# Up-projections of a hybrid decoder step: the first of four weight sums made by a plain and an accumulating transfer

## What is computed

```python
def conv_ffn(x, buf, w_up, conv_w, w_down):
    hc, new_buf = causal_dwconv(x @ w_up, conv_w, buf)     # w_up: (1024, 5632)
    return (jax.nn.silu(hc[..., D_FF:]) * hc[..., :D_FF]) @ w_down, new_buf
```

## Time and profile before

| | |
|---|---|
| median of three runs | 1750.44 us (1749.59 to 1751.86) |
| profiled execution, own time | 1752.5 us |
| its span in the trace | 1749.1 us |
| TensorE busy (matmul) | 1715.6 us, 98% of the span |
| VectorE busy | 1088.8 us, 62% |
| ScalarE busy | 460.1 us, 26% |
| GpSimd busy | 254.5 us, 15% |
| 16 DMA engines | 24% busy, 139.36 MB, 80 GB/s |

### The profile page before, as it was taken

How to read it: one execution, slowest core, us unless ns; L and a number is a source line. 1 busy time by engine, 2 the same in 40 slices (tenths; PEclk the granted TensorE clock), 3 DMA queues, 4 the chain that set the end, 5 groups by cost and what they waited for, 6 DMA issues and landing times. The chain is left out here.

```text
span 1749.1 us, 22019 instructions
## 1 busy us (share of the span) xinstructions
PE 1715.6 (98%) x7827; PEld 1334.3 (76%) x7827; DVE 1088.8 (62%) x2090; ACT 460.1 (26%) x1084; POOL 254.5 (15%) x540
## 2 busy tenths in 40 slices
PE   8999999999899999999999999999999999999999
PEld 6777778877677777777777777777677777777777
DVE  4766775667867666672437655467666667632365
ACT  2433407730422222220014101114222222200051
POOL 0111216762210000000100000002000000001100
PEclk9999999999999999999999999999999999999999
DMA  4232210312122222241130223211222222322211
GB/s 153 73 114 86 80 61 14 110 52 106 48 82 77 83 73 73 85 154 66 67 110 25 96 85 94 73 50 49 61 84 73 73 85 80 129 101 74 82 53 55
DMA packets 45644, 139.36 MB, mean 80 GB/s; under 512 B 4945, under 2 KB 12241, under 8 KB 45537
## 3 DMA queue, kind: packets, MB, share of 16 engines
q1 hardware_dynamic: 42864, 133.36, 23.1%
q10 hardware_dynamic: 2672, 4.61, 0.8%
HBM read 129.63 MB, written 8.31 MB: 79 GB/s over the span
## 5 line engine op out<-in xcount | busy, mean ns | idle before, releaser
L274 PE MATMUL bank<-z,ring 128*128 128x288 f32 x1952 | 508.7, 407 | 6.9 <-DVE z L392 2.3
L274 PEld LDWEIGHTS bank<-z,ring 128*128 128x128 f32 x1952 | 371.1, 191 | 113.4 <-issue 5.1
L274 PE MATMUL bank<-x,ring 128*128 128x288 f32 x1632 | 429.7, 410 | 10.5 <-DMA x<-in_x 4.8
L274 PEld LDWEIGHTS bank<-x,ring 128*128 128x128 f32 x1632 | 311.2, 192 | 101.8 <-issue 6.7
L2188 DVE SCALAR_TENSOR_TENSOR scratch<-scratch 128x592 f32<-128x592 f32 x176 | 146.2, 832 | 25.6 <-ACT scratch L2132 24.0
L274 PE MATMUL bank<-y,ring 128*128 128x288 f32 x616 | 156.7, 406 | 0.3 <-DVE x L1949 0.3
L274 PEld LDWEIGHTS bank<-y,ring 128*128 128x128 f32 x616 | 117.0, 190 | 33.0 <-issue 0.7
L274 PE MATMUL bank<-big,ring 128*128 128x288 f32 x536 | 137.0, 411 | 2.7 <-issue 1.1
L274 PEld LDWEIGHTS bank<-big,ring 128*128 128x128 f32 x536 | 102.4, 192 | 33.1 <-issue 3.4
L2222 POOL COPY scratch<-scratch 128x2 f32<-128x2 f32 x88 | 26.5, 301 | 467.7 <-ACT scratch L2118 467.7
L2132 ACT ACTIVATE scratch<-scratch 128x592 f32<-128x592 f32 x88 | 69.4, 789 | 90.6 <-DVE scratch L2162 89.0
(11 more groups left out here) (377 smaller groups left out, 2236.3 us busy)
## 6 DMA issues: line engine op xcount, KB each, us to landing
ring<-in_w_up SPq DMA_DIRECT2D x88, 512.0 KB, 3.5
ring<-in_w_scin SPq DMA_DIRECT2D x24, 512.0 KB, 3.6
ring<-in_w_qkv SPq DMA_DIRECT2D x21, 512.0 KB, 3.5
ring<-in_w_down SPq DMA_DIRECT2D x12, 704.0 KB, 4.3
scratch<-in_w_down SPq DMA_DIRECT2D x12, 704.0 KB, 5.3
ring<-in_w_z SPq DMA_DIRECT2D x8, 512.0 KB, 3.5
big<-in_st_S SPq DMA_DIRECT2D x16, 256.0 KB, 5.6
out_dn_S_sample<-big SPq DMA_DIRECT2D x16, 256.0 KB, 2.3
```

The lines of the kernel that those rows point to most:

```text
L274: last = pe.matmul(bank[:, 0:HALF], w[:, k * P:(k + 1) * P], rhs(k), start=start and k == 0, stop=k == self.depth - 1, skip_group_check=no ...
```

## The change

s1 of sets 2 to 21 of each layer isn't made by VectorE any more. SP copies a21 from memory to the place of s1 as soon as `p5` of set i - 2 has read the old one (one more 256 KB transfer, ahead of the set's two others). When it has landed (`s1_first`), POOL issues a transfer of a22 from memory that adds to what is there (`accum_op=ALU.add`), which increments `s1_added`. VectorE waits for `s1_added` ahead of `sum2`, and signals `sum1_made` itself behind it. In POOL's queue the transfer for set i stands first in its turn, and `history_out` and `history_in` of a set have moved one turn later in the loop. Sets 0 and 1 keep `sum1`, `sum2` and `sum3`. The names in the diff: `s1_uses` counts the uses of a semaphore.

```diff
--- before.py
+++ after.py
@@ -360,6 +360,14 @@
                 if g >= 2 and not (self.own_blocks and i >= 2):
                     dve.wait_ge(product6, g - 1)
                 dve.tensor_tensor(w["s2"], w["s1"], w["a11"], ALU.subtract).then_inc(sum2_made, 1)
+
+            def sum2_of_loaded(self, dve, i):
+                g, w = self.base + i, self.weights(i)
+                dve.wait_ge(*self.loaded(i, "a11"))
+                dve.wait_ge(*self.loaded(i, "a21"))
+                dve.wait_ge(product6, g - 1)
+                dve.tensor_tensor(w["s2"], w["s1"], w["a11"], ALU.subtract).then_inc(sum2_made, 1)
+                dve.sem_inc(sum1_made, 1)
 
             def sum3(self, dve, i):
                 w = self.weights(i)
@@ -1811,6 +1819,7 @@
             phase_sem(f"ple_{x}") for x in ("projected", "projected_out", "sigmoids", "gate", "out", "p_in"))
         sc_ch, sc_samples, sc_hist, sc_tap0, sc_tap1, sc_conv, sc_made, sc_saved, sc_pads, sc_in = (
             phase_sem(f"sc_{x}") for x in ("ch", "samples", "hist", "tap0", "tap1", "conv", "made", "saved", "pads", "in"))
+        s1_first, s1_added = ([phase_sem(f"s1_{x}{n}") for n in range(2)] for x in ("first", "added"))
         big_loaded = [phase_sem(f"big_loaded{n}") for n in range(4)]
         chunk_loaded = [[phase_sem(f"chunk{s}_{x}_loaded") for x in ("a11", "a12", "a21", "a22")] for s in range(2)]
 
@@ -2800,13 +2809,13 @@
             f.tap(dve, 0, 1, 2)
             f.tap(dve, 0, 0, 1)
             f.tap(dve, 0, 0, 2)
-            d.sum1(dve, 2)
             for i in range(2, FT):
                 p = i - 1
                 if i > 2:
                     f.u2(dve, p)
                 f.c22(dve, p)
-                d.sum2(dve, i)
+                dve.wait_ge(s1_added[i % 2], 16 * s1_uses(layer, i))
+                d.sum2_of_loaded(dve, i)
                 d.sum3(dve, i)
                 f.gate(dve, p - 1)
                 f.c21(dve, p)
@@ -2819,8 +2828,6 @@
                 if p % 2 == 0:
                     down_token(dve, layer, (p - 1) // 2, 1)
                 f.c12(dve, p)
-                if i + 1 < FT:
-                    d.sum1(dve, i + 1)
                 f.tap(dve, p, 0, 1)
                 f.tap(dve, p, 0, 2)
 
@@ -3148,9 +3155,15 @@
             f.history_in(pool, 0)
             f.history_in(pool, 1)
             for i in range(FT):
-                f.history_out(pool, i)
-                if i + 2 < FT:
-                    f.history_in(pool, i + 2)
+                if i >= 2:
+                    pool.wait_ge(s1_first[i % 2], 16 * s1_uses(layer, i))
+                    pool.dma_start(up[layer].weights(i)["s1"], I[f"w_up{layer}"][2 * UP_ORDER[i] + 1][:, ROW // 2:ROW],
+                                   accum_op=ALU.add).then_inc(s1_added[i % 2], 16)
+                if i:
+                    f.history_out(pool, i - 1)
+                    if i + 1 < FT:
+                        f.history_in(pool, i + 1)
+            f.history_out(pool, FT - 1)
 
         def down_pool(pool, layer):
             r, n = residual[2 * layer + 1], norm[2 * layer + 1]
@@ -3194,7 +3207,12 @@
             d, w = up[layer], I[f"w_up{layer}"]
             load_first(sync, dout if layer == 0 else scout, [2 * t for t in UP_ORDER[:2]], w)
             for i in range(2, FT):
+                sync.wait_ge(product5, d.base + i - 1)
+                sync.dma_start(d.weights(i)["s1"], w[2 * UP_ORDER[i] + 1][:, 0:ROW // 2]).then_inc(s1_first[i % 2], 16)
                 load_steady(sync, d, i, 2 * UP_ORDER[i], w)
+
+        def s1_uses(layer, i):
+            return layer * (FT // 2 - 1) + i // 2
 
         def load_chunk(sync, layer, i, block):
             n = ("a11", "a12", "a21", "a22").index(block)
```

## The result

The change makes the kernel slower, by less than was forecast: 1767.2 us (median of 4 runs, 1764.5 to 1768.2) against 1750.2 us, a ratio of 1.0093 with a 95% interval of 1.0076 to 1.0111. The forecast was 1831 us, so 81 us were predicted where 17 came. The profiled execution took 1766.9 us, its span is 1764.7 us: 15.6 us more than the span of before.

What follows compares the result with a forecast made beforehand. TensorE, busy 260.00 of 260.00 us in layer 0's up-projection stage, was taken as the bound. The loss 38 (T - 3.7) + 2 (T - 1.0), 81 us at T = 5.6, on 1750.4 gave 1831.4 us; range 1762 to 1940.

Steps and rivals of the forecast that it cites:

- The bound and the saving: Up-projection stage: TensorE is busy throughout, so the 27 us saved of VectorE's busy time are worth nothing.
- SP's transfer at no cost: SP's queue: the added plain 256 KB load is issued nearly two periods before the sum needs it; cost 0.
- The loop and where the transfer stands in it: POOL's transfer stands behind history_in's copies; last taps, copies, transfer, sum2, p6, u1, taps take 9.9 us and T.
- The rooms: Free time from history_in's copies to sum2's latest start: 4.26 us, or 3.40 with token sums; mean taken as 3.7.
- T: Time from the end of history_in's copies to VectorE's release by POOL's accumulating transfer; taken as 5.6 us.
- 0.1 and 0.2 us taken off for lateness: Steady sets: late sum2 makes c21 late around u1, so free times become 4.16 and 3.20 us.
- Set 2's room: Free time for the transfer at set 2: 0.8 us in layer 0 and 1.2 in layer 1, mean 1.0.
- T = 5.6 us: POOL's accumulating transfer: 3.5 us as a 512 KB load plus 2 us estimated, near the 5.6 median of 256 KB loads.
- the prediction's own formula: Loss over both layers: 38 (T - 3.7) + 2 (T - 1.0) = 40 T - 143 us, 81 us at T = 5.6.
- The clock at nothing: TensorE's granted clock: 12% idle time per period lowers it to 0.98, costing 0.04 us in a period: nothing.
- A: Rival: the transfer fits its room, T under 3.7 us, only set 2 pays; 1753.8 us at T = 2.7; chance 0.10.
- B: Rival: adding or POOL's descriptor making is slow, T 9 us, costing 217 us, 1967 us; chance 0.14.

Runs made afterwards that it cites:

- e1: The changed kernel with POOL issuing the accumulating transfer ahead of history_out and history_in: 1750.8 us against 1750.7 for the kernel before, ratio 0.9998.
- e8: The changed kernel with VectorE making s1 of set 2 and the second pair of token sums behind the last taps: 1751.0 us, ratio 1.0000 to before.
- e2: The changed kernel with VectorE's second pair of token sums moved behind the last two taps: 1759.6 us, ratio 1.0042 to the kernel before.
- e7: The changed kernel with VectorE making s1 of set 2 again, without transfers for it: 1759.5 us, ratio 1.0052 to the kernel before.
- e5: The changed kernel with five small POOL memsets ahead of each accumulating transfer: 1801.1 us, ratio 1.0295 to the kernel before.
- e3: The changed kernel with POOL's transfer copying instead of adding: 1754.1 us, ratio 1.0020 to the kernel before.
- e4: The changed kernel with the second transfer issued by SP, plain, once history_in has signalled: 1754.0 us, ratio 1.0018 to the kernel before.

## Why the prediction was wrong

*The bound and the saving: right.* TensorE bounds the stage; VectorE's s1 was worth nothing. e1 shows it: all the work moved off VectorE, in time, and the time is that of before.

*SP's transfer at no cost: right.* It landed in 3.1 us, and e1 and e8 carry it at no loss. (It is issued about 20 us before sum2 needs it, one and a half periods and not nearly two; nothing rests on that.)

*The loop and where the transfer stands in it: right.* The copies, the transfer, sum2 and p6 follow each other as written, and moving the transfer ahead of the copies takes all of the loss away.

*The rooms: right.* 3.4 us and set 2's are shown by e2, e7 and e8, which close each of them. But the sum took their mean, 3.7, and a straight price in every set "for T over 3.7"; between 3.4 and 4.26 us only every second set pays. At T = 4.0 the two ways come out nearly alike, 38 x 0.32 = 12 us and 18 x 0.62 = 11 us. The 0.1 and 0.2 us taken off for lateness don't show in the change: with T = 3.92 the gap is 0.54, and T less the gap is 3.35 to 3.39 us in 17 of its 18 small gaps. They do show in e5, where every set is late: there T less the gap is 3.2 and 4.2 us in turn in nearly all sets, close to the prediction's 3.20 and 4.16. That it is c21's lateness which takes the difference isn't shown. Set 2's room was 1.6 and 1.2 us in the change instead of a mean of 1.0; in the change, e2 and e5 alike it is p1(2)'s own wait (1.66, 1.26, 0.50, 1.04, 0.83 and 0.99 us) within 0.06 us. With the waits of the kernel before, 0.81 and 1.25, that gives the prediction's 0.8 and 1.2.

*T = 5.6 us: wrong, and this is the step that failed.* It measured 4.02. The prediction put it together from 3.5 us, as for a load of twice the bytes, and 2 us, an estimate without a row, for POOL's part and the slower adding; and it took the median row of the same size, 5.6 us, as agreeing. Neither held. In e3 and e4 POOL's part was 0.15 us and the whole price of adding, the second read included, 1.23 us above a plain transfer: T is 2.64 + 0.15 + 1.23 = 4.02, so beyond the 3.5 us there was 0.5 and not 2. And the row is one of a crowd: 16 transfers issued within 8 us, with the DMA engines almost full while they ran. First a stretch of before with those 16 in flight, then one of the change with a single adding transfer (the last two columns are the DMA share and GB/s):

```profile
335.00:339.00 4.00, 4.00 (x38) 4.00 (x37) 1.41 (x2) 2.93 (x10) 3.94 (x5) 1.00 0.98 349
```

```profile
576.30:580.30 4.00, 4.00 (x18) 3.13 (x17) 0.91 (x2) 0.56 (x2) 1.19 (x4) 1.00 0.44 66
```

66 GB/s in 4.00 us is 264 KB: hardly more than the transfer's own 262 KB, so next to nothing else moved. The row nearer to such a moment was the minimum of rows 10, 2.7 us: e4, SP's plain transfer there, took 2.64.

The sum is steep in T, 40 us for each us, so a miss of 1.6 us became 64 us. With T = 4.02 the prediction's own formula gives 40 x 4.02 - 143 = 18 us, and 17 were measured; with e5's 4.85 it gives 51, and 49 were. That these agree so well is in part luck: the mean room, the clock left out and the shortened groups left out err in different directions and nearly cancel.

*The clock at nothing: wrong, by 1.6 us.* The prediction looked at the period's 12% of idle time, with a loop that holds one product, and not at set 2, the one place where TensorE waits for nearly 3 us in a piece.

*The rivals.* A (T under 3.7) didn't come, but came closer than its chance of 0.10 said: in e3 and e4, with T under 3.4, the time is 1754, as it put it for that case. B was far off. The range, 1762 to 1940, held the result near its lower end, since its lower end stood for T = 3.9; the point itself stood 1.6 us of T too high.

## What to carry to other kernels

When a transfer is issued from a compute engine's queue, look for what it now stands behind in that queue: here one place in the order, two copies (0.33 us together) that wait for the end of the period, was the whole loss of 17 us, and the same traffic one place earlier costs nothing that can be told. Where a loop multiplies an unknown latency by 40, don't take it from the median of a row whose transfers ran in a crowd but, if yours runs alone, from that row's minimum plus what is new, and give the break points on the way (here 3.4 and 4.26 us), since the price changes slope at each. And taking work from an engine with idle time, on a path that another engine bounds, pays nothing even if it succeeds.

## What was unexpected of the hardware

A plain transfer through POOL's software queue was only 0.15 us slower than SP's for 256 KB (T of 2.79 against 2.64). Adding float32 in the transfer costs 1.2 us for 256 KB: POOL's instruction grows from 0.54 to 0.85 us, the packets from 80 to 144 for each transfer, and the share of the 16 engines from 1.8% to 4.0%; T grows with the bytes (2.61, 2.97 and 4.02 us for 64, 128 and 256 KB), the instruction doesn't. The granted clock fell to 0.57 to 0.60 for some 4 us behind single gaps of 2.79, 3.25 and 3.54 us between full-speed products (after shorter ones just before), and stayed full behind one of 2.53 us; each of these falls cost 1.6 us. Behind e5's gaps of 3.92 and 4.22 us it fell too, at 1.5 and 2.4 us. What decides it isn't shown. In each period 1.5 MB instead of 1 MB came in without making another load later: the 512 KB loads landed after 3.5 us with and without.
